# Six extra megabyte buffers for two pairs of experts, and dense weight blocks loaded two by two, in a two-layer hybrid backbone

## The chip, the cores and the metric

One NeuronCore of a Trainium2 chip runs the whole program. The metric is device time in microseconds of one execution; the median of three executions of the kernel before is 1771.43 us (1770.98 to 1771.93).

## What is computed

Two layers of a hybrid backbone on 256 tokens (128 context, 128 latent), model width 1024, all in float32. Each layer is a token-mixing part and a mixture of experts, cut here to what matters:

```python
def layer(x, mod, P, l, ctx=None):
    h = rms_norm(x, P["norm_attn_pre"][l]) * (1 + sc1) + sh1     # sc1, sh1, ... from silu(c) @ w_mod[l] + b_mod[l]
    a, new_ctx = token_mix(h, P, l, ctx)                         # w_in, three attention branches, w_branch, w_out
    x = x + g1 * rms_norm(a, P["norm_attn_post"][l])
    h = rms_norm(x, P["norm_ffn_pre"][l]) * (1 + sc2) + sh2
    x = x + g2 * rms_norm(moe(h, P, l), P["norm_ffn_post"][l])

def moe(h, P, l):     # 64 experts of width 256, top 6 of 64 per token, and one shared expert
    hid = silu(x @ moe_w_gate[l]) * (x @ moe_w_up[l])            # per expert
    routed = (hid * gates) @ moe_w_down[l]
    return routed + shared
```

The weights of one expert are three blocks of one megabyte: two of gate and up, one of down. A layer reads 60 MB of other ("dense") weights and 192 MB of expert weights.

## The kernel before, in words

**The ring.** All large weights go through `ring`, twelve slots of 1 MB (8 KB to each of the 128 partitions). SyncE (SP) issues every load, in the order of use. Before a load it waits on `ring_free`, a counter that TensorE (PE) raises with `release` when the matmul behind the last use of a slot has run. A layer has 60 dense blocks (`LOADS`), one slot and one DMA each (`load`, L345; semaphore `ring_in`, one for each slot), and then 32 pairs of experts, each of three parts of 2 MB (`load_expert`, L356; 16 KB to a partition; semaphore `pair_in`, one for each two slots). So a pair of experts takes six slots, and the ring holds two pairs.

**The other queue.** All other transfers are issued by GpSimd (POOL), in program order. At the start: the constants (L381), the two condition vectors (L382, L383) and the two halves of x (L385, L386). Then POOL waits for both halves of x (`x_in`) before it goes on. In each layer it then issues nine small parameter loads (L401 to L405, semaphore `params_in`), four vectors for lambda (L410) and, after the first modulation rows are staged, the caches and three smaller weights (L413 to L424). Later in the layer it writes the token table to HBM (`h_table`, L461 and L465) and gathers from it the token rows of each pair of experts (L484).

**PE at the start of a layer.** `mod_batch(0)` (L551) needs dense blocks 0 to 3 and, in the first layer, the condition vectors; `mod_batch(1)` needs blocks 4 to 7. PE then waits for `params_in` and transposes the parameters (L501), then the modulation rows, once ACT has staged them, and the normalised x. ACT and VectorE (DVE) turn these into `hT`, and the first projection (L618, blocks 8 and 9) starts. `mod_batch(2)` needs blocks 10 to 13, and so on. At the start of the second layer DVE first adds the result of the experts to x and normalises it (L1377 to L1397, L1389), then copies the parameters (L1409) and forms the modulation (L1426, L1434).

**The experts.** For each pair, PE runs `gate_up` (L1012, 32 matmuls), `down` (L1036, 16), transposes of inputs and hidden rows (L501) and `combine` (L1059), one pair behind. The last of a part's predecessors is released at the first matmuls of the next one. The first pair waits for its gathered rows.

**Scratch.** One buffer `region` of 23,936 words to a partition holds all activations, under views whose lifetimes are laid out by hand.

```python
def load(n, dst, src, base=rounds):
    sp.wait_ge(ring_free, (base + n // RING_SLOTS) * RING_SLOTS + n % RING_SLOTS + 1)
    sp.dma_start(dst, src).then_inc(ring_in[n % RING_SLOTS], 16)
...
pool.wait_ge(start_tr, 1)
apart(pool)
pool.wait_ge(x_in, 32)
pool.sem_inc(x_ready, 2)
...
mod_batch(0)
mod_batch(1)
pe.wait_ge(params_in, (l + 1) * 9 * 16)
transpose(PS[:, 0, 0:PAR_ROWS], prow[:], PAR_ROWS).then_inc(params_tr, 1)
mod_transposes(0, range(4), frees=1)
```

Of the kernel before, what the change touches and what calls it, by code (L numbers as in the profile page):

```python
# [30 lines left out]
P = 128  # L31
D = 1024
KC = D // P
T = 256
DEPTH = 2
# [13 lines left out]
ROW = D + N_EXPERTS  # L49
# [12 lines left out]
ROUNDS = LOADS // RING_SLOTS  # L62
PASS_ROUNDS = EXPERT_LOADS // RING_SLOTS
MOD_BATCH = 4
# [66 lines left out]
def hybrid_layers(nc, a, o):  # L131
    with ExitStack() as ctx:
# [98 lines left out]

        h2x = view(3072, 2, ROW)
        xg = view(9216, XG, ROW)
# [10 lines left out]
        row_i = view(16160, PAIRS).bitcast(U32)  # L244
        shid = view(0, 2, T)
        first_hot = view(1024, 2, P)
        sh_th = view(5248, 2, T)
        sh_rows = view(16384, 2, T)
        partials = view(16896, 2, P)
        h2T = view(17408, KC, T)  # L250

        r_score, r_bias = view(2048, 2, N_EXPERTS), view(2176, 2, N_EXPERTS)
        r_top = view(2304, 2 * N_GROUPS, 8)
        r_gs, r_grep = view(2432, 2, 12), view(2456, 2, 12)
        r_g8, r_gm = view(2480, 2, 8), view(2496, 2, 8)
        r_mask, r_mrep = view(2512, 2, 66), view(2644, 2, 66)
        r_m8, r_sum = view(2776, 2, 8), view(2792, 2)
        r_most, r_np = view(2794, 1), view(2795, 1)

# [3 lines left out]

        ring_in = [sem(f"ring_in{i}") for i in range(RING_SLOTS)]
        pair_in = [sem(f"pair_in{i}") for i in range(0, RING_SLOTS, 2)]
        ring_free = sem("ring_free")
        start_in, consts_in = sem("start_in"), sem("consts_in")
# [67 lines left out]
        @block.sync  # L335
        def _(sp):
            passes = sp.alloc_register("sp_passes")
            sp.reg_mov(passes, 0)
            for l in range(DEPTH):
                rounds = sp.snap(l * ROUNDS + sp.snap(passes, min_val=0, max_val=8) * PASS_ROUNDS)  # L340

                def load(n, dst, src, base=rounds):

                    sp.wait_ge(ring_free, (base + n // RING_SLOTS) * RING_SLOTS + n % RING_SLOTS + 1)
                    sp.dma_start(dst, src).then_inc(ring_in[n % RING_SLOTS], 16)  # L345

                def load_block(n):
                    load(n, ring[:, n % RING_SLOTS, :], blocks[ds(l, 1), n].rearrange("o p w -> p (o w)"))

                for n in range(LOADS):  # L350
                    load_block(n)

                def load_expert(n, pair, part, base):
                    slot = n % RING_SLOTS
                    sp.wait_ge(ring_free, (base + n // RING_SLOTS) * RING_SLOTS + slot + 2)
                    sp.dma_start(ring[:, slot:slot + 2, :].rearrange("p s w -> p (s w)"),  # L356
                                 expert_blocks[ds(l, 1), ds(pair, 1), part].rearrange("o e p w -> p (o e w)")).then_inc(pair_in[slot // 2], 16)

                def experts_pass(base):
                    with sp.Fori(0, PAIRS // 2) as i:  # L360
                        for u in range(2):
                            for part in range(3):
                                load_expert(6 * u + 2 * part, i * 2 + u, part, base + i)

                experts_pass(rounds + ROUNDS)

                sp.wait_ge(npass_ready, l + 1)
                apart(sp)
                npass = sp.value_load(npass_i[0:1, 0:1], min_val=1, max_val=4)
                with sp.If(npass > 1):  # L370
                    with sp.Fori(1, npass) as p:
                        experts_pass(rounds + ROUNDS + p * PASS_ROUNDS)
                    sp.nop()
                sp.reg_add(passes, passes, npass)
                sp.nop()
# [121 lines left out]
        def _(pe):  # L497
# [15 lines left out]
            for l in range(DEPTH):  # L513
# [3 lines left out]
                def arrived(n):  # L517

                    pe.wait_ge(ring_in[n % RING_SLOTS], (l * ROUNDS + n // RING_SLOTS + 1) * 16)

# [464 lines left out]
                with pe.Fori(0, npass) as p:  # L985
                    q = pe.snap(before_l + p)
                    base = pe.snap(q * PASS_ROUNDS)
                    done = pe.snap(q * N_EXPERTS)
                    pairs = pe.snap(q * PAIRS)
                    pe_gathers = [pe.snap(q * (16 * len(range(i, PAIRS, XG)))) for i in range(XG)]  # L990

                    def transpose_lists():
# [8 lines left out]
                    def gate_up(g):  # L1001

                        pe.wait_ge(xe_ready, done + (2 * g + 2))
                        for k in range(KC):
                            if g == 0 and k == 3:
                                transpose_lists()
                            for e in range(2):
                                n = 6 * g + 2 * (k // 4) + e
                                if k % 4 == 0 and e == 0:
                                    arrived_pair(n, base)  # L1010
                                w = ring[:, n % RING_SLOTS, :].rearrange("p (k c) -> p k c", k=4)
                                last = pe.matmul(PS[e * CAP:(e + 1) * CAP, 0, :], xe[:, k, e * CAP:(e + 1) * CAP], w[:, k % 4, :],  # L1012
                                                 start=(k == 0), stop=(k == KC - 1), skip_group_check=True)
                                if e == 0 and (k == 4 or (k == 0 and g >= 1)):
                                    release(last, 2)
                        last.then_inc(gu_done, 1)
# [9 lines left out]
                    def down(g):  # L1026
                        arrived_pair(6 * g + 4, base)
                        pe.wait_ge(hidT_ready, pairs + (g + 1))
                        if g >= 1:

                            pe.wait_ge(og_ready, done + 2 * g)
                        for half in range(2):
                            for f in range(2):
                                for e in range(2):
                                    w = down_slot(6 * g + 4 + e)
                                    last = pe.matmul(PS[e * CAP:(e + 1) * CAP, 2 + half, :], hid[:, f, e * CAP:(e + 1) * CAP],  # L1036
                                                     w[:, f, half * HALF:(half + 1) * HALF], start=(f == 0), stop=(f == 1), skip_group_check=True)
                            last.then_inc(down_done, 1)

                    def transpose_inputs(g, half, frees=0):  # L1040
# [6 lines left out]
                        for c in range(4):  # L1047
                            last = transpose(PS[:, bank, c * P:(c + 1) * P], xg[:, g % XG, (4 * half + c) * P:(4 * half + c + 1) * P])
                            if c == 0 and frees:
                                release(last, frees)  # L1050
                        last.then_inc(xe_tr, 1)
# [784 lines left out]
```

## Time and profile before

| | |
|---|---|
| median of three executions | 1771.43 us |
| the profiled execution | 1772.09 us |
| its span, from the first to the last instruction | 1770.3 us |
| PE busy | 1679.5 us (95%) |
| HBM read | 576.02 MB |
| first layer / its experts | 0 to 890 us / 396 to 890 us |
| second layer / its experts | 890 to 1770 us / 1262 to 1770 us |

The profiled execution is 0.66 us above the median; 1.8 us of it lie outside the span. "To landing" is the time from the issue of a DMA to its completion.

### The profile page before, as it was taken

Reading aid. Unit: us, or ns where it says so; the run is one execution under the profiler, and the core shown is the slowest. Engines: PE = TensorE matmul, PEld = TensorE weight load, DVE = VectorE, ACT = ScalarE, POOL = GpSimd, SP = SyncE. Lnnn points to the kernel's source line nnn. Section 1 sums busy time; section 2 is a strip of 40 time slices with the busy share of each in tenths; the row PEclk is TensorE's granted clock in tenths of the full one; section 3 lists DMA queues with packets and bytes.
Section 4 is the critical chain, followed back from the end, with each engine's and each line's share of the span. In section 5 each row is a group of like instructions: output and inputs, shape, how many; then the busy total and the mean of one; then the engine's idle time right before and its main releaser. Section 6 shows DMA issues by size and latency. Waiting matters only on the chain.

```text
span 1770.3 us, 20981 instructions
## 1 busy us (share of the span) xinstructions
PE 1679.5 (95%) x8083; PEld 898.9 (51%) x8083; DVE 429.3 (24%) x1168; ACT 321.8 (18%) x754; POOL 119.4 (7%) x161
## 2 busy tenths in 40 slices
PE   4999998979999999999989999999699999999996
PEld 2877787543333333333368878784233333333332
DVE  1115444351111111111131444434311111111112
ACT  1010341121111111111120113302111111111111
POOL 3001000010000000001010000001100000000000
PEclk9999998989999999999999999999899999999998
DMA  9994222358999999999999633234599999999992
GB/s 352 419 382 154 96 95 98 130 188 312 427 423 426 426 423 425 427 426 424 419 399 403 246 105 103 88 125 166 213 410 424 426 426 425 425 425 424 426 426 96
DMA packets 60204, 559.87 MB, mean 316 GB/s; under 512 B 12908, under 2 KB 13056, under 8 KB 20176
## 3 DMA queue, kind: packets, MB, share of 16 engines
q1 hardware_dynamic: 44928, 528.50, 72.6%
q0 software_dynamic: 15184, 30.07, 5.0%
q8 instruction: 66, 1.08, 0.2%
q14 instruction: 26, 0.21, 0.0%
HBM read 576.02 MB, written 4.78 MB: 328 GB/s over the span
## 4 chain that ended last, share of the span: by engine, by line
PE 91%; DMA 5%; DVE 2%; issue 1%; ACT 1%; SPq 0%; POOL 0%; POOLq 0%; DVEq 0%; PEldq 0%
PE PS L1012 25%; PE PS L600 14%; PE PS L1036 13%; PE PS L1059 12%; PE PS L501 6%; PE PS L838 5%; DMA ring<-in_blocks 4%; PE PS L886 3%; PE PS L551 2%; PE PS L665 2%; DMA region<-h_table,region 1%; PE PS L924 1%; PE PS L824 1%; PE PS L944 1%; PE PS L618 1%; PE PS L728 1%
## 5 line engine op out<-in xcount | busy, mean ns | idle before, releaser
L1012 PE MATMUL PS<-ring,region 128*64 128x512 f32 x2048 | 455.3, 597 | 3.0 <-ACT region L1280 1.6
L1012 PEld LDWEIGHTS PS<-ring,region 128*64 128x64 f32 x2048 | 148.1, 138 | 295.3 <-issue 295.2
L600 PE MATMUL PS<-region,ring 128*128 128x256 f32 x1088 | 245.3, 381 | 0.0
L1059 PE MATMUL PS<-region 128*128 128x512 f32 x512 | 241.0, 594 | 0.0
L1036 PE MATMUL PS<-ring,region 128*64 128x512 f32 x1024 | 235.2, 601 | 1.0 <-DVE region L1734 1.0
L600 PEld LDWEIGHTS PS<-region,ring 128*128 128x128 f32 x1088 | 203.8, 190 | 33.5 <-issue 6.3
L1716 DVE SCALAR_TENSOR_TENSOR region<-region,PS 128x256 f32<-128x256 f32 x64 | 27.0, 421 | 668.8 <-ACT region L1287 668.8
L501 PE MATMUL PS<-const,region 128*128 128x128 f32 (+1 forms) x925 | 140.2, 282 | 45.0 <-DMA region<-h_table,region 16.8
L501 PEld LDWEIGHTS PS<-const,region 128*128 128x128 f32 (+1 forms) x925 | 108.1, 143 | 145.7 <-issue 73.7
L1036 PEld LDWEIGHTS PS<-ring,region 128*64 128x64 f32 x1024 | 68.1, 137 | 159.3 <-issue 157.8
L1291 ACT ACTIVATE region<-PS 128x512 f32<-128x512 f32 x128 | 76.4, 597 | 273.4 <-PE PS L1036 273.4
L484 POOL DMA_INDIRECT region<-h_table,region x64 | 63.6, 994 | 858.7 <-DVE region L1721 772.6
L1059 PEld LDWEIGHTS PS<-region 128*128 128x128 f32 x512 | 87.4, 190 | 65.4 <-issue 64.4
L1280 ACT ACTIVATE region<-PS 128x512 f32<-128x512 f32 x128 | 76.4, 597 | 147.7 <-PE PS L501 147.7
L1287 ACT ACTIVATE region<-PS 128x256 f32<-128x256 f32 x64 | 24.5, 383 | 410.4 <-PE PS L1012 410.4
L838 PE MATMUL PS<-region,ring 128*128 128x256 f32 x384 | 86.9, 387 | 1.4 <-DVE region L1605 1.4
L838 PEld LDWEIGHTS PS<-region,ring 128*128 128x128 f32 x384 | 73.5, 193 | 13.0 <-DVE region L1605 2.2
L551 PE MATMUL PS<-ring,condT 128*32 128x256 f32 x768 | 49.0, 412 | 16.4 <-DMA ring<-in_blocks 16.4
L1721 DVE SCALAR_TENSOR_TENSOR region<-PS,region 64x256 f32<-64x256 f32 x128 | 61.9, 484 | 4.3
L886 PE MATMUL PS<-ring,region 128*128 128x512 f32 x128 | 55.3, 592 | 0.0
L1730 DVE TENSOR_SCALAR region<-const,region 128x256 f32<-128x256 f32 x64 | 22.6, 353 | 106.6 <-PE PS L1059 106.5
L551 PEld LDWEIGHTS PS<-ring,condT 128*32 128x32 f32 x768 | 26.6, 118 | 38.4 <-issue 26.5
(255 smaller groups left out, 993.1 us busy)
## 6 DMA issues: line engine op xcount, KB each, us to landing
ring<-in_expert_blocks SPq DMA_DIRECT2D x192, 2048.0 KB, 17.0
ring<-in_blocks SPq DMA_DIRECT2D x120, 1024.0 KB, 18.1
region<-post_rows POOLq DMA_DIRECT2D x8, 512.0 KB, 4.9
h_table<-region POOLq DMA_DIRECT2D x4, 512.0 KB, 3.9
region<-in_w_kvk POOLq DMA_DIRECT2D x2, 640.0 KB, 13.6
region<-in_mla_w_ukv POOLq DMA_DIRECT2D x2, 512.0 KB, 16.9
region<-in_post_pack POOLq DMA_DIRECT2D x2, 512.0 KB, 20.4
region<-h_table,region POOLq DMA_INDIRECT x64, 10.7
```

The lines of the kernel that those rows point to most:

```text
L484: pool.indirect_dma_start(xg[:, g % XG, :], None, table, bass.IndirectOffsetOnAxis(ap=row_i[:, g:g + 1], axis=0), bounds_check=T - 1, oob_ ...
L501: return pe.transpose(out, in_, ident[0:n, 0:n])
L551: last = pe.matmul(PS[32 * g:32 * g + 32, MOD_BANK[group], half * 256:half * 256 + 256], condT[:, k, :], w[:, k, :], start=(k == 0), stop= ...
L600: last = pe.matmul(PS[:, j % 2, m * T:(m + 1) * T], w[:, k, m * P:(m + 1) * P], hT[:, k, :], start=(k == 0), stop=(k == KC - 1))
L838: last = pe.matmul(PS[:, b + n // 2, (n % 2) * T:(n % 2 + 1) * T], w[:, k, jj * P:(jj + 1) * P], src[:, k, :], start=(k == 0), stop=(k == 3))
L886: last = pe.matmul(PS[:, 4 + 2 * t + half, :], merged[:, k, t * P:(t + 1) * P], w[:, k % 4, :], start=(k == 0), stop=(k == KC - 1))
L1012: last = pe.matmul(PS[e * CAP:(e + 1) * CAP, 0, :], xe[:, k, e * CAP:(e + 1) * CAP], w[:, k % 4, :], start=(k == 0), stop=(k == KC - 1), s ...
L1036: last = pe.matmul(PS[e * CAP:(e + 1) * CAP, 2 + half, :], hid[:, f, e * CAP:(e + 1) * CAP], w[:, f, half * HALF:(half + 1) * HALF], start ...
L1059: last = pe.matmul(PS[:, 4 + 2 * t + half, :], hot[:, t * P:(t + 1) * P], og[:, half * HALF:(half + 1) * HALF], start=False, stop=True, sk ...
L1280: act.activation(xe[:, 4 * half:4 * half + 4, :].rearrange("p k s -> p (k s)"), bank(3 if g == 0 and half else 1), ACT.Copy).then_inc(xe_r ...
L1291: act.activation(og[:, half * HALF:(half + 1) * HALF], bank(2 + half), ACT.Copy).then_inc(og_ready, 1)
L1721: ve.scalar_tensor_tensor(out=hid_rows[rows], in0=PS[rows, 0, 2 * P:4 * P], scalar=xg[rows, g % XG, D + 2 * g + e:D + 2 * g + e + 1], in1= ...
```

## The change

The ring stays. Six further megabytes are kept in `region` for two of the 32 pairs of experts, numbers 2 and 17, whose parts then take no ring slots: parts 0 and 1 at words 0 to 8191 (one DMA of 2 MB each), part 2 at 17408 and 21760 (two DMAs of 1 MB). Pair 2 is loaded before the experts begin, in three steps between ring loads, each behind semaphores that say that the space is free. Pair 17 is loaded behind the ring loads of pair 16, once PE is done with pair 2 (`spare_used`). Some small views (`h2x`, the shared expert's hidden rows, the router's scratch) move to make room. The dense blocks are packed two by two on the host, so that each DMA brings two neighbouring slots, 2 MB, with 16 KB to a partition; SP waits until both are free, and PE waits for the two together. Cut to its core:

```diff
-PASS_ROUNDS = EXPERT_LOADS // RING_SLOTS
+SPARE_PAIRS = (2, 17)
+PASS_ROUNDS = (EXPERT_LOADS - 6 * len(SPARE_PAIRS)) // RING_SLOTS
...
-                for n in range(LOADS):
-                    load_block(n)
+                def load_two(n, src, base):
+                    slot = n % RING_SLOTS
+                    sp.wait_ge(ring_free, (base + n // RING_SLOTS) * RING_SLOTS + slot + 2)
+                    sp.dma_start(ring[:, slot:slot + 2, :].rearrange("p s w -> p (s w)"), src).then_inc(pair_in[slot // 2], 16)
+                for n in range(0, LOADS, 2):
+                    load_two(n, blocks[ds(l, 1), n // 2].rearrange("o p w -> p (o w)"), rounds)
...
+                def load_spare(pair, part):
+                    if part < 2:
+                        sp.dma_start(view(4096 * part, 4096), pair_block(pair, part)).then_inc(spare_in[part], 16)
+                    else:
+                        for e in range(2):
+                            sp.dma_start(spare[part][e], pair_block(pair, part)[:, 2048 * e:2048 * (e + 1)]).then_inc(spare_in[part], 16)
+                def experts_pass(base, q):
+                    for n in range(0, 8, 2):
+                        load_expert(n, n // 6, n % 6 // 2, base)
+                    sp.wait_ge(merged_ready, (l + 1) * KC)
+                    load_spare(SPARE_PAIRS[0], 0)
+                    sp.wait_ge(xn_tr, (l + 1) * 8)
+                    load_spare(SPARE_PAIRS[0], 1)
+                    load_expert(8, 1, 1, base)
+                    sp.wait_ge(state_out, (l + 1) * 6 * 16)
+                    sp.wait_ge(router_done, (l + 1) * 2)
+                    sp.wait_ge(shared_gu, (l + 1) * 2)
+                    load_spare(SPARE_PAIRS[0], 2)
+                    load_expert(10, 1, 2, base)
+                    load_pairs(3, 14, 12, base)
+                    sp.wait_ge(spare_used, sp.snap(q * 2) + 1)
+                    for part in range(3):
+                        load_spare(SPARE_PAIRS[1], part)
+                    load_pairs(18, 14, 8 * RING_SLOTS, base)
...
                 def arrived(n):
-                    pe.wait_ge(ring_in[n % RING_SLOTS], (l * ROUNDS + n // RING_SLOTS + 1) * 16)
+                    arrived_pair(n, rounds)
...
+                    def weights_of(g, part, e, k):
+                        w = spare[part][e] if g in SPARE_PAIRS else ring[:, in_ring(g, part) % RING_SLOTS + e, :]
+                        return w.rearrange("p (k c) -> p k c", k=k)
```

## Rows read from the trace of the kernel before

**Rows 1.** PE's waits over the span: total us, times, longest us.

```profile
PE PS L501 <- DMA region<-h_table,region: 16.8, 2, 8.6
PE PS L551 <- DMA ring<-in_blocks: 16.4, 4, 6.7
```

**Rows 2.** Chain that ended last, in the first layer's experts: start us, us, what.

```profile
720.16 6.87 PE PS L1012 x32
...
735.29 6.87 PE PS L1012 x32
```

**Rows 3.** Ring loads to landing, in stretches 330:400, 420:440 and 800:860.

```profile
DMA to landing us min/median/max: 7.8/7.9/8.1
...
DMA to landing us min/median/max: 9.2/11.1/13.3
...
DMA to landing us min/median/max: 20.0/21.7/24.4
```

**Rows 4.** PE's timeline, both layers' starts: start us, us, instructions, [idle before].

```profile
17.36 4.90 PE L551 MATMUL PS<-ring,condT 128*32 128x256 f32 x64 [5.35 <-DMA ring<-in_blocks]
29.00 5.90 PE L551 MATMUL PS<-ring,condT 128*32 128x256 f32 x64 [6.73 <-DMA ring<-in_blocks]
34.83 0.28 PE L501 MATMUL PS<-const,prow 68*128 68x68 f32 x1
...
39.08 14.05 PE L618 MATMUL PS<-region,ring 128*128 128x256 f32 x64 [0.99 <-ACT region L1124]
...
897.39 5.20 PE L551 MATMUL PS<-ring,condT 128*32 128x256 f32 x64 [4.12 <-DMA ring<-in_blocks]
...
906.78 3.48 PE L618 MATMUL PS<-region,ring 128*128 128x256 f32 x15 [0.99 <-ACT region L1124]
```

**Rows 5.** DVE's timeline at the second layer's start.

```profile
900.64 0.75 DVE L1389 TENSOR_SCALAR region<-xr,roots 128x1024 f32<-128x1024 f32 x1
902.84 0.23 DVE L1409 COPY parT<-PS 128x68 f32<-128x68 f32 x1 [1.45 <-PE PS L501]
...
904.57 0.18 DVE L1434 SCALAR_TENSOR_TENSOR pre<-modT,parT 128x16 f32<-128x16 f32 x1
```

**Rows 6.** PE's timeline, first layer: the end of the shared expert's gate and up.

```profile
367.95 7.03 PE L924 MATMUL PS<-ring,region 128*128 128x512 f32 x16
```

**Rows 7.** Gathers issued at 386.53 and 427.17: us to landing.

```profile
region<-h_table,region POOLq DMA_INDIRECT x1, 7.0
...
region<-h_table,region POOLq DMA_INDIRECT x1, 11.1
```

**Rows 8.** Page, SP's DMA queue: packets, MB, share of 16 engines.

```profile
q1 hardware_dynamic: 44928, 528.50, 72.6%
```

**Rows 9.** POOL's timeline, first layer's start: issue us, us to issue it.

```profile
2.99 0.57 POOL L385 DMA_DIRECT2D xr<-in_x_prompt  x1
...
19.93 0.54 POOL L401 DMA_DIRECT2D prow<-in_b_mod  x1 [15.84 <-DMA xr<-in_x_sample]
```

**Rows 10.** POOL's transfers issued 2.49 to 3.55: KB, us to landing.

```profile
xr<-in_x_prompt POOLq DMA_DIRECT2D x1, 512.0 KB, 12.4
xr<-in_x_sample POOLq DMA_DIRECT2D x1, 512.0 KB, 15.6
...
region<-in_c POOLq DMA_DIRECT2D x1, 4.0 KB, 9.1
```

**Rows 11.** First and last of nine parameter loads, issued 19.93 and 24.32.

```profile
prow<-in_b_mod POOLq DMA_DIRECT2D x1, 24.0 KB, 5.1
...
lamc<-in_lam_consts POOLq DMA_DIRECT2D x1, 1.0 KB, 6.4
```

**Rows 12.** The same two for the second layer, issued 836.71 and 840.90.

```profile
prow<-in_b_mod POOLq DMA_DIRECT2D x1, 24.0 KB, 9.5
...
lamc<-in_lam_consts POOLq DMA_DIRECT2D x1, 1.0 KB, 16.4
```

**Rows 13.** Window behind the first gather: busy, clock (1.00 full), DMA share, GB/s.

```profile
396.30:401.70 5.40, 5.38 (x14) 1.33 (x15) 0.00 (x0) 0.00 (x0) 0.00 (x0) 0.50 0.02 3
```

More of the change, by code:

```diff
@@ L230, in hybrid_layers @@
         moe_scaled = view(6144, 2, D)
[L232 removed]
+        h2x = view(12480, 2, ROW)
         xg = view(9216, XG, ROW)
@@ L250, in hybrid_layers @@
         h2T = view(17408, KC, T)
[L252 to L258, printed above, removed]
+        r_score, r_bias = view(8192, 2, N_EXPERTS), view(8320, 2, N_EXPERTS)
+        r_top = view(8448, 2 * N_GROUPS, 8)
+        r_gs, r_grep = view(8576, 2, 12), view(8600, 2, 12)
+        r_g8, r_gm = view(8624, 2, 8), view(8640, 2, 8)
+        r_mask, r_mrep = view(8656, 2, 66), view(8788, 2, 66)
+        r_m8, r_sum = view(8920, 2, 8), view(8936, 2)
+        r_most, r_np = view(8938, 1), view(8939, 1)
+        spare = [[view(at, 2048) for at in pair] for pair in ((0, 2048), (4096, 6144), (17408, 21760))]
         def norm_scratch(at, n):
             return [region[:, at + i * n:at + (i + 1) * n] for i in range(3)]
-        ring_in = [sem(f"ring_in{i}") for i in range(RING_SLOTS)]
+        ring_free = sem("ring_free")
+        spare_in = [sem(f"spare_in{i}") for i in range(3)]
         pair_in = [sem(f"pair_in{i}") for i in range(0, RING_SLOTS, 2)]
-        ring_free = sem("ring_free")
+        spare_used = sem("spare_used")
         start_in, consts_in = sem("start_in"), sem("consts_in")
@@ L361, in experts_pass, with load_pairs @@
+                def load_pairs(first, count, n, base):
+                    with sp.Fori(0, count // 2) as i:
                         for u in range(2):
                             for part in range(3):
-                                load_expert(6 * u + 2 * part, i * 2 + u, part, base + i)
-                experts_pass(rounds + ROUNDS)
+                                load_expert(n + 6 * u + 2 * part, i * 2 + (first + u), part, base + i)
+                def experts_pass(base, q):
[16 more added lines that the diff above has]
+                    load_pairs(18, 14, 8 * RING_SLOTS, base)
@@ L990, in _, with in_ring, landed, used @@
                     pe_gathers = [pe.snap(q * (16 * len(range(i, PAIRS, XG)))) for i in range(XG)]
+                    spare_twice = [pe.snap(q * 64 + 32 * i) for i in (1, 2)]
+                    spare_once = [pe.snap(q * 32 + 16 * i) for i in (1, 2)]
+                    def in_ring(g, part):
+                        return 6 * (g - sum(g > s for s in SPARE_PAIRS)) + 2 * part
+                    def landed(g, part):
+                        if g not in SPARE_PAIRS:
+                            arrived_pair(in_ring(g, part), base)
+                        else:
+                            use = SPARE_PAIRS.index(g)
+                            pe.wait_ge(spare_in[part], spare_twice[use] if part == 2 else spare_once[use])
+                    def weights_of(g, part, e, k):
+                        w = spare[part][e] if g in SPARE_PAIRS else ring[:, in_ring(g, part) % RING_SLOTS + e, :]
+                        return w.rearrange("p (k c) -> p k c", k=k)
+                    def used(g, last):
+                        if g not in SPARE_PAIRS:
+                            release(last, 2)
                     def transpose_lists():
@@ L1049, in transpose_inputs @@
                             if c == 0 and frees:
-                                release(last, frees)
+                                used(g - 1, last)
                         last.then_inc(xe_tr, 1)
```

49 lines of the change are left out of this document (26 added, 23 removed).

## The prediction

> **What bounds the kernel now.** I read the page's busy shares first: PE is busy 95% of the span, so only PE's waits can be won. The view of waits gives them all at once: 16.4 us in four waits for dense ring blocks and 16.8 us in two waits for the first gather of a layer [rows 1]. No wait for an expert block is among them. The chain of waits says the same: in the expert part, pair follows pair every 15.13 us (720.16 to 735.29), matmuls only [rows 2].
>
> The queue of loads is another matter. A 2 MB load lands 7.9 us after its issue before the experts begin, 11.1 us at their start and 21.7 us near their end (medians) [rows 3]. The DMA engines are a little slower than PE's demand and fall behind by 21.7 - 11.1 = 10.6 us in some 400 us, 0.4 us per pair. The ring, two pairs or 30.3 us deep, absorbs it until the layer ends. There the debt shows once: the second layer's mod_batch(1) waits 4.12 us for block 7 and then runs 5.20 us. The other three ring waits are at the program's start, 5.35 and 6.73 us for blocks 3 and 7 [rows 4] and the rest of the 16.4, where no buffer can help: nothing is loaded yet.
>
> **What the spare buffers give.** Pair 2 is read early, while the DMA engines have room, and during its use (15.1 us) no ring load is asked for. So the queue empties, loads start again at 7.9 instead of 11.1 us to landing, and the debt at the layer's end is 3.2 us less. That nearly covers the 4.12 us. Pair 17 costs and gives nothing: its 6 MB are asked for ahead, but the queue is busy then, so the bytes only change places; one pair later no ring load is asked for.
>
> What then is late next? DVE. At the second layer's start it ends the second half of the normalised x at 900.64 + 0.75 = 901.4 whatever PE does: that work hangs on the last combine, not on blocks. From its copy of the parameters to the end of `pre` it takes 904.75 - 902.84 = 1.9 us, of which some 0.5 us is a wait for PE that would go. So `pre` is there at 901.4 + 1.4 = 902.8, and the projection starts 2.0 us behind it as now (904.75 to 906.78), at 904.9 [rows 4, 5]. **Gain: 1.9 us.** The wait seems to offer more: 4.12, and 5.20 against the 3.66 us that such a batch takes at full clock, 5.7 in all. Bounds: 0 and 5.7. Behind the second layer's experts comes nothing, so its debt never shows.
>
> **What the early loads of pair 2 cost.** Parts 0 and 1 go out behind the branches and behind the last transposes of x. SP is held there with ring loads behind it, but those need slots that PE releases later than it raises these semaphores, in the shared expert. Part 2 goes out at the end of the shared gate and up, 375.0 [rows 6], with one ring load ahead of it: at most 4 MB, 10 us, so it ends near the first gather's issue at 386.53, which is on PE's path. That gather takes 7.0 us now; one in a full queue takes 11.1 [rows 7]. Bounds for a layer: 0 and 4.1. I take 0.25, as only the tail of part 2 can meet it: **cost 0.5 us** for both layers. The moved views add no wait, and PE reads the same bytes from another address: 0.
>
> **What loading dense blocks by twos costs at the start.** The bytes are the same, and PE waits for blocks 0 to 3 and 4 to 7 together anyway: 0.
>
> But POOL's transfers share the DMA engines, and how they share is in the count of packets. Rows of 120 dense loads and 192 expert loads, and one closing packet on each of 16 engines for each load, are 120 x 128 + 192 x 128 + 312 x 16 = 44,928, exactly queue 1's count. So a row is one packet, of 8 KB in a dense block and 16 KB in an expert's. The queue moved 528.50 MB in 72.6% of 1770.3 us, 411 GB/s or 25.7 KB per us and engine [rows 8]: 8 KB take 0.32 us, 16 KB 0.64. The two halves of x land at 2.99 + 12.4 = 15.4 and, issued 0.57 us later, at 3.56 + 15.6 = 19.2 us, 3.8 us apart [rows 9, 10]. Each has 8 rows of 4 KB to an engine, 0.16 us each, and 8 x (0.16 + 0.32) = 3.8. So each POOL row takes turns with one row of the ring's, and beside 16 KB rows half an x takes 8 x (0.16 + 0.64) = 6.4 us.
>
> From that step follows:
> - The constants (8 rows to an engine) land 8 x 0.32 = 2.6 us later, the condition vectors (four turns, row and closing packet twice) 1.3 more: 2.5 + 9.1 = 11.6 [rows 10] becomes 15.5. mod_batch(0) starts at 17.36 [rows 4] and needs them some 1.5 us before: it stays.
> - x: another 2 x 2.6 us. 19.2 becomes 28.2, **9.0 us later**. POOL issues the nine parameter loads only behind x, so from 28.9 instead of 19.93 [rows 9].
> - These nine land from 19.93 + 5.1 = 25.0 to 24.32 + 6.4 = 30.7 now [rows 11], and PE takes them at 34.83 [rows 4]: 4.1 us of cover. The second layer shows the same nine beside 16 KB rows: from 836.7 + 9.5 = 846.2 to 840.9 + 16.4 = 857.3, 11.1 us for eight, 1.4 each, where two turns make 1.3 [rows 12]. (The first lay behind a gather there, so its 9.5 is not used.) After the change: the first at 28.9 + 5.1 + 0.6 = 34.6, the last 10.2 to 11.1 us later, 44.8 to 45.7 instead of 30.7. I take the lower, as these are turns and nothing else.
> - mod_batch(1) ends at 34.8 as now, and PE then stands idle for 10 us. The parameters' transpose moves from 34.83 to 44.9; of the way from there to the projection, 4.25 us, the 0.6 us that PE spends on waiting for ACT's staging is over by then. The projection starts 9.5 us later. Blocks 8 to 15 have landed by then, so nothing is caught up.
> - PE's clock will have fallen. The nearest row is the first gather's wait of 8.2 us: behind it the clock was 0.50, 1.2 GHz, and 12 matmuls took 5.4 us [rows 13] where 12 of 32 in 6.87 us take 2.6 [rows 2]: 2.8 us lost. The batch behind the 6.73 us wait took 5.90, 2.2 more than 3.66 [rows 4]. I take 2.5; bounds 0 and 3.
>
> **Cost: 12.0 us**, bounds 6 (x and the parameters only half as late) and 15. In the second layer the parameters are loaded beside 16 KB rows already, and no cache or weight of POOL's is among PE's waits [rows 1]: 0.
>
> **Sum.** 12.0 + 0.5 - 1.9 = +10.6 us. Against the profiled execution's 1772.09 us that is 1782.7; it stands 0.66 us above the median, and on the median the sum is 1771.43 + 10.6 = 1782.0 us.
>
> The Trainium skill, "DMA: Bandwidth & Descriptors", "Queues, rings and completion order", has the same turn-taking: a DMA engine drains a whole packet of one ring before it switches. But its section "SWDGE vs HWDGE vs iDMA" has a packet of at most 4096 B preferably; by that a 16 KB row would cost POOL no longer turns than an 8 KB row, the start would stay as it is, and the first rival below is the result. The packet count of [rows 8] speaks against it.
>
> **Rivals.**
> 1. *The turns do not grow with the row.* POOL's transfers keep their times, and -1.9 + 0.5 is left: 1770.0 us. For it: the nine loads of [rows 12] had a gather ahead of them, which may have made them slow. Against: once the first had landed, the others still came 1.4 us apart, and 0.7 in the first layer [rows 11]. Chance 0.15.
> 2. *Faster: the debt at the layer boundary decides.* The start is as in 1, block 7 lands before 893.3, and DVE's chain moves forward as well, so that all of 5.7 us is won: 1765.7 us. It decides from the point where DVE is done before PE's batch. For it: the ring wait is real and the debt falls. Against: DVE's timeline [rows 5]. Chance 0.10.
> 3. *Slower still: the first gathers are late too.* Part 2 of pair 2 and the ring load beside it make each take 11.1 us, +8.2 less the 0.5 counted: 1789.7 us. Against: part 2 goes out 11 us ahead of the gather. Chance 0.05.
>
> Should the change not do what it says, with no debt won, 1.9 us are missing from the gain: 1783.9 us, inside the forecast's own range.
>
> **The numbers.** The forecast, slower by the start, has 0.70, with a range of its own from 1776 to 1787 (6 to 15 us at the start, the rest as summed). A measurement of this kernel can tell about 0.2%, 3.5 us, from no change. Rival 1 lies within that, rival 2 is faster, rival 3 slower: faster 0.10, same 0.15, slower 0.75. The 8-in-10 range reaches from rival 1's case to most of the forecast's own: 1769 to 1786.
>
> **What would show it.** x_sample lands near 28 us instead of 19.2; POOL's first parameter load goes out at 28.9; PE is idle from 34.8 to about 45, released by a parameter's DMA; the first projection starts near 48.6 instead of 39.1, at half clock. At the second layer's start no ring wait is left, and the projection comes 1.9 us sooner behind the last combine. Ring loads of pairs 3 to 5 land in about 8 us. The period of the experts stays 15.13 us. I am wrong if x lands before 22 us, if the projection starts before 43, or if a wait for a ring part appears among the experts.

## The result and the profile after

The changed kernel takes 1781.76 us (median of 5 runs, 1779.11 to 1783.82). The kernel before, run beside it, takes 1771.21 us (1770.79 to 1771.93). The ratio is 1.0058, with an interval of 1.0047 to 1.0069: slower by 10.5 us. The forecast was 1782.0. The profiled execution took 1781.76 us, with a span of 1780.0, 9.7 us more than the span before.

PE's waits in the changed kernel (total us, times, longest us), which answer to [rows 1]:

```profile
PE PS L534 <- DMA region<-h_table,region: 16.6, 2, 8.4
PE PS L534 <- DMA region<-in_c: 15.6, 1, 15.6
PE PS L534 <- DMA lamc<-in_lam_consts: 10.2, 1, 10.2
...
PE PS L584 <- DMA ring<-in_blocks: 7.9, 2, 4.5
```

A wait of 10.2 us for the last of the nine parameter loads is new. The ring waits are down from 16.4 to 7.9 us, but that is mostly no gain: PE now waits 15.6 us for the condition vectors and 1.6 us for what DVE makes of them, and blocks 0 to 3 are there by then. The gather waits are as before.

PE's timeline at the first layer's start, beside [rows 4] (start us, us, instructions, [idle before]):

```profile
17.43 6.36 PE L584 MATMUL PS<-ring,condT 128*32 128x256 f32 x64 [1.58 <-DVE condT L1401]
28.26 6.07 PE L584 MATMUL PS<-ring,condT 128*32 128x256 f32 x64 [4.46 <-DMA ring<-in_blocks]
44.50 0.37 PE L534 MATMUL PS<-const,prow 68*128 68x68 f32 x1 [10.16 <-DMA lamc<-in_lam_consts]
44.67 4.47 PE L534 MATMUL PS<-const,region 128*128 128x128 f32 x20
48.99 14.68 PE L651 MATMUL PS<-region,ring 128*128 128x256 f32 x64
```

The first batch starts where it did (17.43, before 17.36). The parameters' transpose starts at 44.50 instead of 34.83, and the projection at 48.99 instead of 39.08: 9.9 us later. It takes 14.68 instead of 14.05 us; from 44.5 to 49.0 the granted clock was 0.50, and from 49.0 to 54.0 it was 0.87. At the end of the projection PE is 10.5 us late. It stays 10.2 us late from then on, as the kernel before waits a little for the next ring blocks:

```profile
53.31 3.66 PE L551 MATMUL PS<-ring,condT 128*32 128x256 f32 x64 [0.17 <-DMA ring<-in_blocks]
```

So the start accounts for a loss of 10.2 us, which is about the whole.

What POOL does in that time, beside [rows 9], and the landing of its transfers, beside [rows 10, 11] (KB, us from issue to landing):

```profile
3.55 0.54 POOL L419 DMA_DIRECT2D xr<-in_x_sample  x1
28.59 0.54 POOL L434 DMA_DIRECT2D prow<-in_b_mod  x1 [24.50 <-DMA xr<-in_x_sample]
...
32.98 0.68 POOL L438 DMA_DIRECT2D lamc<-in_lam_consts  x1
```

```profile
xr<-in_x_prompt POOLq DMA_DIRECT2D x1, 512.0 KB, 18.7
xr<-in_x_sample POOLq DMA_DIRECT2D x1, 512.0 KB, 24.3
...
region<-in_c POOLq DMA_DIRECT2D x1, 4.0 KB, 13.0
...
prow<-in_b_mod POOLq DMA_DIRECT2D x1, 24.0 KB, 5.9
...
lamc<-in_lam_consts POOLq DMA_DIRECT2D x1, 1.0 KB, 11.5
```

The halves of x land at 2.98 + 18.7 = 21.7 and 3.55 + 24.3 = 27.9 us, 6.2 apart where they were 3.8 apart. The parameters land from 28.59 + 5.9 = 34.5 to 32.98 + 11.5 = 44.5, 10.0 us for eight, 1.25 each. The ring's queue shows the longer rows in its packets (packets, MB, share):

```profile
q1 hardware_dynamic: 36864, 528.50, 72.1%
```

That is 256 loads of 128 rows and 16 closing packets each: 60 dense pairs, 180 ring loads of experts, and for the spares 8 whole parts and 8 halves of a part.

At the second layer's start the ring wait stands yet, beside 4.12 and 906.78 in [rows 4]:

```profile
895.98 3.66 PE L584 MATMUL PS<-ring,condT 128*32 128x256 f32 x64
903.03 5.35 PE L584 MATMUL PS<-ring,condT 128*32 128x256 f32 x64 [3.39 <-DMA ring<-in_blocks]
...
912.53 12.76 PE L651 MATMUL PS<-region,ring 128*128 128x256 f32 x58 [0.98 <-ACT region L1185]
```

From mod_batch(0) to the projection PE takes 912.53 - 895.98 = 16.55 us; before, that batch started at 889.62, and the same way took 906.78 - 889.62 = 17.16. So 0.6 us were won here, where 1.9 were forecast.

The ring loads to landing show why (stretches 345:410, 435:470 and 800:860, beside [rows 3]), and so do the windows of the time in which pair 2 is used (us; PE, PEld, DVE, ACT, POOL busy; PE's clock, DMA share, GB/s):

```profile
DMA to landing us min/median/max: 7.4/7.7/9.7
...
DMA to landing us min/median/max: 7.6/9.2/10.9
...
DMA to landing us min/median/max: 19.6/21.5/23.9
```

```profile
440.00:450.00 10.00, 10.00 (x46) 4.16 (x42) 1.81 (x4) 1.58 (x3) 0.99 (x1) 1.00 0.79 309
450.00:460.00 10.00, 10.00 (x46) 3.21 (x46) 0.35 (x1) 1.19 (x2) 0.00 (x0) 1.00 0.17 35
```

The kernel before has a DMA share of 1.01 in both windows. The three spare parts, 6.3 MB, were loaded ahead, 14.8 us of transfer at 424 GB/s. But while PE reads them it frees no slot, and the DMA engines stand idle for 0.21 x 10 + 0.83 x 10 = 10.4 us. The queue then takes some time to come back to its full rate. Here is the stretch behind the pause, first the changed kernel, then the kernel before:

```profile
460.00:480.00 20.00, 20.00 (x89) 8.34 (x86) 3.98 (x9) 4.35 (x8) 1.98 (x2) 1.00 0.95 380
...
460.00:480.00 20.00, 20.00 (x90) 7.38 (x88) 2.17 (x5) 3.96 (x7) 0.99 (x1) 1.00 1.00 424
```

Over 460 to 510 us the rates are 398 and 425 GB/s. That is 1.35 MB less, or another 3.2 us. So what the buffers hold ahead is spent by then: 14.8 - 10.4 - 3.2 leaves 1.2 us. Near the layer's end a ring load takes 21.5 us to land, and took 21.7.

**Clock.** Most of the rest of the difference between the two profiles lies in stretches in which both do the same work at different clocks. The third number from the end is the granted clock (1.00 is 2.4 GHz, 0.50 is 1.2). The kernel before:

```profile
262.00:286.00 24.00, 19.91 (x109) 14.83 (x109) 10.42 (x33) 7.48 (x21) 1.24 (x3) 0.79 0.12 44
...
1136.00:1146.00 10.00, 6.99 (x37) 4.65 (x38) 6.85 (x24) 3.14 (x10) 0.00 (x0) 0.85 0.18 48
```

The changed kernel, in the same work:

```profile
272.00:296.00 24.00, 19.86 (x117) 15.00 (x117) 10.42 (x33) 7.49 (x21) 1.60 (x3) 0.93 0.14 49
...
1144.00:1154.00 10.00, 8.02 (x35) 5.67 (x34) 5.93 (x21) 2.12 (x6) 0.00 (x0) 0.56 0.00 0
```

Matmul by matmul, the changed kernel is 10.2 us late after the start and 8.8 at the end of the first gather's wait, with more clock in the attention. It is 6.4 us late behind the first pair of experts, in which 12 matmuls took 4.53 instead of 5.39 us. It is 5.8 behind the layer boundary, 7.6 at 1150 (less clock), and 9.7 from the second layer's first pairs to the end, where 12 matmuls took 5.39 instead of 4.47. Over the five runs of the changed kernel the mean granted clock goes from 0.980 in the fastest (1779.11 us) to 0.977 in the slowest (1783.82). In which stretches those runs differ isn't on record.

### The profile page after: what moved, and what is told of

It reads as the page before. It is cut to its first block, busy times and chain, and to the rows that moved or that the text cites. A ratio compares the mean times of both kernels' runs of the same rounds, so it can differ in the third digit from the quotient of the medians.

```text
span 1780.0 us, 20799 instructions
## 1 busy us (share of the span) xinstructions
PE 1683.9 (95%) x8083; PEld 902.4 (51%) x8083; DVE 429.4 (24%) x1168; ACT 321.9 (18%) x754; POOL 119.4 (7%) x161
## 4 chain that ended last, share of the span: by engine, by line
PE 91%; DMA 4%; DVE 2%; issue 1%; ACT 1%; POOL 0%; POOLq 0%; DVEq 0%
PE PS L1069 25%; PE PS L633 13%; PE PS L1097 13%; PE PS L1120 12%; PE PS L534 6%; PE PS L871 4%; PE PS L919 3%; PE PS L584 2%; PE PS L651 2%; PE PS L698 2%; DMA xr<-in_x_sample 1%; PE PS L957 1%; DMA ring<-in_blocks 1%; PE PS L977 1%; PE PS L857 1%; DMA region<-h_table,region 1%
## 5 line engine op out<-in xcount | busy, mean ns | idle before, releaser
L1069 PE MATMUL PS<-ring,region 128*64 128x512 f32 x1920 | 427.2, 597 | 3.2 <-ACT region L1341 1.7
L1069 PEld LDWEIGHTS PS<-ring,region 128*64 128x64 f32 x1920 | 138.9, 138 | 277.3 <-issue 277.2
L1097 PE MATMUL PS<-ring,region 128*64 128x512 f32 x960 | 220.6, 602 | 1.0 <-DVE region L1795 1.0
L534 PE MATMUL PS<-const,region 128*128 128x128 f32 (+1 forms) x925 | 142.2, 285 | 48.0 <-DMA region<-h_table,region 16.6
L1097 PEld LDWEIGHTS PS<-ring,region 128*64 128x64 f32 x960 | 63.9, 137 | 149.4 <-issue 147.9
L1250 ACT ACTIVATE region<-PS,negm 128x128 f32<-128x128 f32 (+1 forms) x96 | 39.0, 415 | 37.8 <-DVE negm L1601 20.0
## 6 DMA issues: line engine op xcount, KB each, us to landing
ring<-in_expert_blocks SPq DMA_DIRECT2D x180, 2048.0 KB, 16.4
```

Of the source, the lines that this page charges most:

```text
L534: return pe.transpose(out, in_, ident[0:n, 0:n])
```

## The experiments

The seven kernels were run in two groups, each with its own runs of the kernel before. Experiments 1, 2, 3 and 7 stand beside 1770.55 us (median of 29 runs), 4, 5 and 6 beside 1772.1 us (23 runs). Ratios are to the kernel before of the same group. They weigh all runs, so they aren't the quotients of these medians: experiment 3, for one, would be at 1.0029 by the medians.

**1. The dense pairs alone** (e3_pairs_only). The kernel before, with the blocks packed and loaded two by two:

```diff
-                for n in range(LOADS):
-                    load_block(n)
+                for n in range(0, LOADS, 2):
+                    slot = n % RING_SLOTS
+                    sp.wait_ge(ring_free, (rounds + n // RING_SLOTS) * RING_SLOTS + slot + 2)
+                    sp.dma_start(ring[:, slot:slot + 2, :].rearrange("p s w -> p (s w)"),
+                                 blocks[ds(l, 1), n // 2].rearrange("o p w -> p (o w)")).then_inc(pair_in[slot // 2], 16)
```

> The kernel before with the dense blocks by twos alone (16 KB rows), no spare buffers. My theory: the whole loss is here, 1781.5 us (1779 to 1785), x_sample at 28, projection at 49. If the spare buffers have a part in the loss, it is below 1778.

Measured: 1780.66 us, ratio 1.0051 (1.0034 to 1.0067). The start is the changed kernel's:

```profile
45.36 0.38 PE L504 MATMUL PS<-const,prow 68*128 68x68 f32 x1 [10.70 <-DMA lamc<-in_lam_consts]
```

As expected, the loss is in the pairs: 9.0 us by the ratio, and a projection that starts at 49.85. The spare buffers have no part in it that the runs can show.

**2. The spare buffers alone** (e2_spares_only). The changed kernel, the dense blocks one by one in rows of 8 KB as before.

```diff
-                for n in range(0, LOADS, 2):
-                    load_two(n, ...)
+                for n in range(LOADS):
+                    sp.wait_ge(ring_free, (rounds + n // RING_SLOTS) * RING_SLOTS + n % RING_SLOTS + 1)
+                    sp.dma_start(ring[:, n % RING_SLOTS, :], ...).then_inc(ring_in[n % RING_SLOTS], 16)
```

> The spare buffers alone, dense blocks one by one as before. My theory: start as before, the second layer's ring wait shorter by about 0.7 us (3.4 instead of 4.1), time 1770.5 us (1769.5 to 1771.5). If early loads of pair 2 or the moved views cost something of their own beside the start, the time is above 1772; if the full 5.7 us at the layer boundary are to be had, it is near 1766.

Measured: 1772.22 us, ratio 1.0002 (0.9991 to 1.0014). The projection starts at 37.70, and a ring wait of 1.73 us behind it takes the 1.4 us back. The boundary wait is 3.13 us. The median lies outside the expected 1769.5 to 1771.5, and above the 1772 that was to show a cost of the buffers' own; the ratio to its own group shows neither a cost nor a gain.

**3. Pairs, but rows of 8 KB** (e1_rows8). One DMA still brings two blocks and PE still waits for the two; only the layout in memory is the old one, so a partition's 16 KB come as two rows.

```diff
-                    load_two(n, blocks[ds(l, 1), n // 2].rearrange("o p w -> p (o w)"), rounds)
+                    sp.dma_start(ring[:, slot:slot + 2, :], blocks[ds(l, 1), n:n + 2].rearrange("o s p w -> p (o s) w")).then_inc(pair_in[slot // 2], 16)
```

> The change with one edit: the two dense blocks of a load are still one DMA of 2 MB with PE and SP waiting for both, but their rows are 8 KB again. If POOL's turns grow with the ring's row (my theory), the start is that of the kernel before: x_sample lands at 19 to 20 us, the first projection starts at 39 to 40, and the time is 1770.5 us (1769.5 to 1772). If it is the size of the DMA or the waiting for two slots, x_sample stays near 28 and the time near 1781.8.

Measured: 1775.77 us, ratio 1.0023 (1.0012 to 1.0034), 4 us slower than before where I had expected none. x_sample lands at 3.55 + 16.5 = 20.1 us, and PE's timeline shows the length of the row and the pairing apart:

```profile
xr<-in_x_sample POOLq DMA_DIRECT2D x1, 512.0 KB, 16.5
```

```profile
38.29 14.05 PE L653 MATMUL PS<-region,ring 128*128 128x256 f32 x64 [0.99 <-ACT region L1187]
52.27 3.66 PE L586 MATMUL PS<-ring,condT 128*32 128x256 f32 x64
59.78 5.26 PE L664 MATMUL PS<-region,ring 128*128 128x256 f32 x16 [3.85 <-DMA ring<-in_blocks]
```

The projection starts at 38.29, so the 10 us are back (39.08 before): the length of a row did it. But once the start isn't late, a wait of 3.85 us appears at block 14, which is read alone and now has to wait for block 15. It isn't SP's wait for two free slots: the load goes out at 23.84, where block 14 went out at 23.19 before. But its two blocks land together at 59.7, where block 14 landed at 56.9 and block 15 at 60.7. Behind the wait, block 14's 16 matmuls take 5.26 instead of 3.72 us. In the changed kernel this price is hidden behind the 10 us.

**4. Only the first sixteen blocks as before** (e4_first16_alone). The changed kernel, with blocks 0 to 15 of a layer loaded and waited for one by one, as 8 KB halves of the same pairs; from 16 on pairs with 16 KB rows.

```diff
-                for n in range(0, LOADS, 2):
+                for n in range(16):
+                    sp.wait_ge(ring_free, (rounds + n // RING_SLOTS) * RING_SLOTS + n % RING_SLOTS + 1)
+                    half = slice(n % 2 * 2048, n % 2 * 2048 + 2048)
+                    sp.dma_start(ring[:, n % RING_SLOTS, :], blocks[ds(l, 1), n // 2].rearrange("o p w -> p (o w)")[:, half]).then_inc(ring_in[n % RING_SLOTS], 16)
+                for n in range(16, LOADS, 2):
```

> The changed kernel, but the first 16 dense blocks of a layer are loaded one by one in rows of 8 KB (halves of the same pairs), and PE waits for each alone; the blocks from 16 on stay in pairs with rows of 16 KB. My theory (only the turns that stand beside the loads of x and of the parameters count, and the pairing costs PE 3.6 us where block 14 waits for block 15): x_sample lands near 20 us, no wait for the parameters (lamc) over 1 us, projection starts within 1 us of the kernel before, 1771 us in all (1769 to 1774). Rival (long rows and pairs cost wherever they stand in the dense part): 1777 or more, with new waits for the ring after the projection has started.

Measured: 1771.71 us, ratio 1.0005 (0.9993 to 1.0017). x_sample lands at 3.55 + 15.9 = 19.5 us, there is no wait for a parameter, and block 14 isn't waited for:

```profile
38.60 14.05 PE L663 MATMUL PS<-region,ring 128*128 128x256 f32 x64 [0.99 <-ACT region L1197]
52.58 3.66 PE L596 MATMUL PS<-ring,condT 128*32 128x256 f32 x64
56.17 3.72 PE L674 MATMUL PS<-region,ring 128*128 128x256 f32 x16
```

Both prices belong to a layer's first sixteen blocks. The other forty-four of sixty can come in long rows at no cost, and at no gain, that the runs can show.

**5. The parameters ahead of the wait** (e6_params_first). The changed kernel, but in the first layer POOL issues the nine parameter loads before it waits for x.

```diff
             pool.wait_ge(start_tr, 1)
             apart(pool)
-            pool.wait_ge(x_in, 32)
-            pool.sem_inc(x_ready, 2)
...
                 pool.dma_start(lamc[:], at_layer(a["lam_consts"], l).broadcast_to([P, 2])).then_inc(params_in, 16)
+                if l == 0:
+                    pool.wait_ge(x_in, 32)
+                    pool.sem_inc(x_ready, 2)
```

> The changed kernel, but POOL issues the nine small parameter loads of the first layer before it waits for x, so that they go behind x in the queues instead of after it. My theory (the delay is POOL's wait for x, which lands at 27.8 us, and then nine small loads one turn behind the other): the last parameter lands near 39 us instead of 44.5, the projection starts near 43.5 instead of 49.0, 1776.5 us in all (1774 to 1780). Rival (the turns of 16 KB set the landing of the small loads whatever the order): the last parameter still lands near 44 us, 1781.8 us. Rival (x is pushed back by the small loads): x_sample lands later than 30 us and the time stays over 1780.

Measured: 1776.34 us, ratio 1.0022 (1.0008 to 1.0035), near the 1776.5 expected. The last parameter, issued at 21.35 instead of 32.98, lands at 39.8 instead of 44.5:

```profile
xr<-in_x_sample POOLq DMA_DIRECT2D x1, 512.0 KB, 24.4
...
lamc<-in_lam_consts POOLq DMA_DIRECT2D x1, 1.0 KB, 18.4
```

```profile
39.82 0.38 PE L535 MATMUL PS<-const,prow 68*128 68x68 f32 x1 [6.52 <-DMA lamc<-in_lam_consts]
...
44.31 14.22 PE L652 MATMUL PS<-region,ring 128*128 128x256 f32 x64
```

x isn't pushed back, and the projection starts 4.7 us sooner. So half of the loss was POOL's wait for x. The other half is the parameters' turns behind x's: x_sample lands at 28.0, the first parameter, issued at 17.21, at 28.6, and the last 11.1 us after that, 1.4 us each.

**6. Rows of 4 KB** (e7_rows4_before). The kernel before, each dense block as two rows of 4 KB to a partition.

```diff
-                    load(n, ring[:, n % RING_SLOTS, :], blocks[ds(l, 1), n].rearrange("o p w -> p (o w)"))
+                    load(n, ring[:, n % RING_SLOTS, :].rearrange("p (h w) -> p h w", h=2),
+                         blocks[ds(l, 1), n].rearrange("o h p w -> p (o h) w"))
```

> The kernel before, with the dense blocks in rows of 4 KB (two per partition and block) and nothing else changed. My theory (a small load takes one turn behind each row of the busy queue, and the turn's length goes with the row): x_sample takes about 14.5 us instead of 15.6 from issue to landing at the least, as low as 11 if the turn is nearly all of it; the first small parameter loads 3 to 4 us instead of 5.1; 61,000 packets or so in the ring's queue. The time stays within 0.2% of 1771 us, since the projection isn't held by x alone. Rival (short rows cost bandwidth): ring loads of the start land later, and the time is 1774 us or more.

Measured: 1776.56 us, ratio 1.0031 (1.0019 to 1.0043).

```profile
xr<-in_x_prompt POOLq DMA_DIRECT2D x1, 512.0 KB, 9.8
xr<-in_x_sample POOLq DMA_DIRECT2D x1, 512.0 KB, 12.0
...
lamc<-in_lam_consts POOLq DMA_DIRECT2D x1, 1.0 KB, 5.3
```

The turns of x behave as expected: its halves land 2.8 us apart (8 x (0.16 + 0.16) = 2.6 by the forecast's sum), the condition vectors 1.3 us sooner. The first parameter load takes 4.9 us, where 3 to 4 were expected and 5.1 were measured before. The packets are 60,288, (120 x 2 + 192) x 128 + 312 x 16. The time isn't as expected. It is the rival's (1774 us or more), but not by the rival's reason alone:

```profile
18.25 5.80 PE L552 MATMUL PS<-ring,condT 128*32 128x256 f32 x64 [7.58 <-DMA ring<-in_blocks]
33.26 5.13 PE L552 MATMUL PS<-ring,condT 128*32 128x256 f32 x64 [9.21 <-DMA ring<-in_blocks]
```

```profile
20.00:25.00 5.00, 4.05 (x52) 2.01 (x44) 1.15 (x3) 0.00 (x0) 3.47 (x7) 1.00 1.03 380
25.00:30.00 5.00, 0.00 (x0) 0.00 (x0) 0.00 (x0) 0.00 (x0) 0.00 (x0) 0.95 1.07 179
```

Block 7 lands at 33.1 instead of 28.9. From 25 to 30 us the DMA engines are busy all the time and move only 179 GB/s. Before, that slump came behind block 7 (361 GB/s in 25:30 and 161 in 30:35); now POOL is through with x sooner, its small loads go out at 16.3 instead of 19.93, and the slump comes ahead of block 7. From 5 to 20 us the rate is 412 to 418 GB/s instead of 420 to 425, so the shorter rows themselves cost little. By 30 us this kernel has moved 1.33 MB less than the one before, 3.1 us at 424 GB/s, and 2.1 of them fall into 25:30: the slump has the larger share. Block 7 is also issued later, at 7.1 instead of 4.8 us, but the DMA engines had work without a break all the same.

The trace's packets say whose slump it is. In 30:35 of the kernel before, 64% of the engines' time goes to packets of 2048 B, at a median of 776 ns each; in 25:30 others of the same size took a median of 86 ns. They belong to five loads of 32 KB each, which repeat one short row for all 128 partitions: the router bias, one of the nine, and the four lambda vectors. The other eight of the nine have smaller packets, and while the first of these are moved, in 20:25, the rate is 408 GB/s.

**7. The spare buffers for pairs 16 and 31** (e5_late_spares). As experiment 2, but the spares hold pair 16, loaded before the experts, and pair 31, the last of a layer, so that ring slots come free for the next layer's blocks a pair sooner.

```diff
-SPARE_PAIRS = (2, 17)
+SPARE_PAIRS = (16, 31)
```

> As the spares alone, but the buffers serve pair 16 (loaded before the experts, as pair 2 was) and pair 31 (loaded behind pair 18). My theory of the debt: six megabytes read early are lost again if the queue runs empty while the spare pair is used, as it did for 10 us beside pair 2; beside pair 16 the queue is 8 to 9 us long, so only some 6 us are lost, ring loads near the end land in 13 to 16 us instead of 22, and block 7 of the second layer is there in time: no ring wait at the boundary. Then DVE's chain binds: the projection starts 17.2 to 17.4 us behind the last combine's end in the kernel before minus 1.9, and the time is 1769.3 us (1768.5 to 1770.5). Rival: DVE does not bind and 5.7 us come, 1765.5. Other rival: the debt is not what delays block 7, and the ring wait stays at 3 to 4 us.

Measured: 1773.18 us, ratio 1.001 (0.9997 to 1.0023).

```profile
890.03 7.11 PE L587 MATMUL PS<-ring,condT 128*32 128x256 f32 x128
897.08 0.28 PE L537 MATMUL PS<-const,prow 68*128 68x68 f32 x1
899.23 1.81 PE L537 MATMUL PS<-const,region 128*128 128x128 f32 x12 [1.88 <-ACT region L1201]
901.96 1.97 PE L537 MATMUL PS<-const,region 128*128 128x128 f32 x8 [0.92 <-DVE region L1453]
905.15 10.11 PE L654 MATMUL PS<-region,ring 128*128 128x256 f32 x33 [1.22 <-ACT region L1188]
```

```profile
905.00:915.00 10.00, 9.85 (x33) 8.27 (x34) 0.80 (x3) 1.05 (x4) 0.70 (x2) 0.71 1.00 320
```

The boundary's ring wait is gone altogether, both batches run through at full clock, and PE then waits for ACT and DVE instead. The projection starts 905.15 - 890.03 = 15.1 us behind mod_batch(0) where it was 17.16, so 2.0 us were won; the forecast had said that DVE leaves 1.9. DVE is what binds: it works without a pause from 889.6 to 903.1, when `pre` is there. In the 10 us behind those waits the clock is 0.71 (1.00 before), and the whole projection takes 16.80 us instead of 14.05. So more than the 2 us is given back: from mod_batch(0) to the end of the projection it is 31.9 us, and was 31.1. That is one profiled execution.

The time missed the expected 1768.5 to 1770.5, and so did the loads near the end: they were to land in 13 to 16 us, and those issued from 842 to 866 us took a median of 23.1. That isn't a sign of less loaded ahead. Block 0 of the second layer goes out at 845.9 instead of 860.7, as pair 31 takes no slots, and waits in the queue for longer. While pair 16 was used, from 650 to 670, the DMA engines stood idle for 5.1 us (the expectation had some 6), against 10.4 beside pair 2.

## Why the prediction was right

**The start: right, in mechanism and size.** Each step against its measurement: condition vectors at 15.5 us (15.6); x_prompt and x_sample 6.4 us apart (6.2); x_sample at 28.2 (27.9); the first parameter load issued at 28.9 (28.59); the last landing at 44.8 to 45.7 (44.5); the transpose at 44.9 (44.50); the projection at 48.6 (48.99), 9.5 us late (9.9). Experiments 1, 2 and 4 show that the pairs of the first blocks do it, experiment 3 that it is the length of their rows and not the pairing, experiment 5 that it runs by POOL's wait and the parameters' turns, and experiment 6 that x's turns follow the row downwards as well. What rival 1 says, that turns don't grow with the row, is refuted.

The prediction's own rows left open what one turn is. Each half of x has eight rows to an engine, and so has a block or a pair in long rows. So one turn for each row and one turn for each whole load both give 3.8 us beside single blocks and 6.4 beside pairs. The runs decide it. In experiment 3 a load still has 2 MB, in 16 rows of 8 KB to an engine, and the halves of x land 3.9 us apart. In experiment 6 a block has 16 rows of 4 KB, and they land 2.8 us apart. Eight rows for eight would fit these too, but not the nine parameter loads: they landed one by one, 0.9 to 2.3 us apart, where eight rows of 16 KB take 5.1 us. So the turns were of one row. That is where the page that the prediction cites needs care: the Trainium skill's "DMA: Bandwidth & Descriptors", "Queues, rings and completion order", has the switch between rings at the end of a packet, but gives such a packet about 9 to 17 descriptors, and no run here shows turns of that size. And the packet of at most 4096 B, which the same page, "SWDGE vs HWDGE vs iDMA", calls preferable, stands there under the descriptors that GpSimd builds. The ring's loads are SP's, and the count has their 16 KB rows as one packet each, so the trace doesn't bear out the use that the prediction made of it.

**The clock at the start: sized about right, put in the wrong place.** The forecast had 2.5 us (0 to 3) behind the start of the projection. Measured, PE ran the 20 transposes of x at half clock (4.47 us; 2.40 where the clock is full, as in experiment 4's start), 2.1 us, and the projection took another 0.6 (14.68 instead of 14.05). But the transposes' 2.1 us filled the time in which PE otherwise waits for ACT (0.58 and 0.99 us in experiment 4): from the parameters' transpose to the projection it is 4.49 us, and was 4.25. So the clock cost 0.9 us on the path, and the start 10.5 us up to the end of the projection, 10.2 for good, not 12.0.

**The cost of 0 for waiting for two blocks: right only under cover.** Experiment 3 shows 3.85 us at block 14. The changed kernel has no wait there, as PE comes 10 us later.

**The boundary: 0.6 us instead of 1.9 between the two profiles.** The step that failed is "the debt at the layer's end is 3.2 us less": the ring wait fell by 0.7 us only. The prediction saw that the queue empties, and counted it as a benefit. It did not set against it what the windows show, 10.4 us in which the DMA engines stand idle ahead of a long stretch in which they fall behind, and 3.2 us lost at less than the full rate behind that; of the 14.8 us loaded ahead that leaves 1.2. The packets of SP's queue say the same. When PE starts pair 2, 90.8 MB have landed instead of 84.7; at pair 4 it is 97.8 instead of 96.6, at pair 8 121.7 instead of 121.5, and at the second layer's mod_batch(0) 272.3 instead of 272.0. Those 0.3 MB are 0.7 us at 424 GB/s, which is what the wait fell by. In experiment 7 it is 276.0 MB at that point, and the wait is gone. Two signs that the prediction named failed with this step: a ring wait is left (3.39 us), and the loads of pairs 3 to 5 land in 9.2 us, not in about 8. Over all profiled kernels the ring wait at the boundary, and the way from mod_batch(0) to the projection, were (us; in the last column the first 12 matmuls of the first pair, which tell its clock):

```
                 spares    ring wait   to the projection   12 matmuls
before           none        4.12         17.16              5.39
experiment 1     none        4.87         19.23              4.50
experiment 6     none        5.08         19.37              4.48
changed          2, 17       3.39         16.55              4.53
experiment 2     2, 17       3.13         16.30              4.37
experiment 3     2, 17       3.06         16.23              4.13
experiment 4     2, 17       3.51         16.68              4.63
experiment 5     2, 17       3.54         16.71              4.43
experiment 7     16, 31      none         15.12              5.39
```

The profile of before belongs to an execution in which 12 matmuls of the first pair ran at half clock. In the two other kernels without early spares they ran faster, and PE waited longer at the boundary. Among equals the early spares take 1.6 us off the wait, and 2.8 off the way (some of it clock behind a shorter wait). The forecast's 1.9 lies between 0.6 and 2.8. Two profiles on one side are few, and no whole time shows the gain (experiment 2: 1.0002). By the bytes landed at mod_batch(0), 272.2 to 272.3 MB with early spares and 271.7 to 272.0 without, about 1 us of the 1.6 isn't explained and stays open. That DVE is next is shown: experiment 7, with an equally slow first pair as before, comes to the projection 2.0 us sooner and no more. With this rival 2 is out as well, which had 5.7 us won once block 7 is there in time.

**The gathers: 0.** 16.6 us in two waits, and 16.8 before; the 0.5 us were not spent. Rival 3 is out.

**The sum.** Forecast: 12.0 + 0.5 - 1.9 = 10.6. Measured between the two profiles: 10.2 at the start, -1.7 in the attention and -2.4 in the first pair by the clock, -0.6 at the boundary, +1.9 and +2.3 by the clock in the second layer, and small ones, 9.7 in all. The clock's four shifts are in no term of the forecast; they nearly cancel, and that is chance. That the median came within 0.3 us of the forecast is luck in part: the start was 1.8 too high and the gathers 0.5, the boundary's gain was 1.3 too high and sets off part of that, and the profile of before, from which the 9.7 is counted, stands 0.66 us above its median. By whole times the pairs alone cost 9.0 us (1.0051, interval 6.0 to 11.9), the spares nothing that the runs can show.

No version was found that beats the kernel before. Experiments 2 and 4 equal it, and have nothing to show for their 6 MB of spare buffers.

## What to carry to other kernels

In this kernel two queues shared the DMA engines, and each gave way to the other for one packet at a time, which was a whole row, up to 16 KB. So the rows of a bulk stream set how long small, urgent transfers of another queue take. A layout that halved the number of loads brought x_sample from 15.6 to 24.3 us and the last parameter from 6.4 to 11.5. Keep rows short beside urgent loads, and make them long later. A spare buffer helps only as far as the load queue has work during its use. Beside pair 2 it hadn't, and all but 1.2 of the 14.8 us loaded ahead were lost within the next pairs; beside pair 16 the queue stood idle for 5.1 us, and the boundary's wait went. And before a wait is taken away, look at which engine ends next, and what PE's clock does if it then waits in small pieces.

## What was unexpected in the hardware

- Five small loads have a price of their own for the bulk stream: while POOL's router bias and lambda vectors landed, the DMA engines were fully busy and moved 161 to 179 GB/s instead of 420. Most of that time went to their packets of 2048 B, with a median of 776 ns instead of 86. When that slump falls has a part in which ring block is late (experiment 6, 4.3 us on block 7). Beside rows of 16 KB it is shallower: 321 GB/s at the least, in 45:50 of the changed kernel.
- Shorter turns aren't better on the whole: rows of 4 KB brought x 3.6 us sooner and made the kernel 5.5 us slower by the ratio.
- PE's clock can take back what a removed wait brings: 2.0 us were won at the boundary in the profile of experiment 7, the next 10 us ran at 0.71, and the projection took 2.75 us more.
